# Two transformer blocks in float32 on one core: the RWKV stage in finer parts and another order

## The reference

```python
feat = feat + (prev - feat) * mu
r, k, v, wl, al, gl = jnp.split(feat, splits, axis=-1)
w = -jax.nn.softplus(-(w0 + jnp.tanh(wl) @ w2)) - 0.5
a = jax.nn.sigmoid(a0 + al @ a2)
g = jax.nn.sigmoid(gl) @ g2
kk = heads(k * k_k);  kk = kk * lax.rsqrt(jnp.sum(kk * kk, -1, keepdims=True) + 1e-12)
k = k * (1.0 + (a - 1.0) * k_a)
decay = jnp.exp(-jnp.exp(heads(w)))
def step(state, inp):
    sa = jnp.einsum('bhvk,bhk->bhv', state, -kk_t)
    state = state * d_t[:, :, None, :] + sa[..., None] * b_t[:, :, None, :] + v_t[..., None] * k_t[:, :, None, :]
    return state, jnp.einsum('bhvk,bhk->bhv', state, r_t)
# y: group norm, lnx_g, lnx_b, plus bonus = sum(r * k * r_k) * v, all times g
x = x + jnp.concatenate([mla_out, rw_out], axis=-1) @ w_o
```

## Time and profile before

| | |
|---|---|
| median of three runs | 2431.26 us |
| the profiled execution | 2428.68 us |
| its span, first to last instruction | 2426.8 us |
| mean granted clock of TensorE | 0.985 |
| busy: PE, DVE, ACT, POOL | 95%, 51%, 31%, 27% |
| chain that ended last: PE, DVE, DMA, issue, ACT | 82%, 8%, 4%, 3%, 2% |
| granted clock by fortieths of the span, in tenths | 9, but 8 in the sixth to eighth |

### The profile page before, as it was taken

How to read it: one execution, slowest core, us unless ns; L and a number is a source line. 1 busy time by engine, 2 the same in 40 slices (tenths; PEclk the granted TensorE clock), 3 DMA queues, 4 the chain that set the end, 5 groups by cost and what they waited for, 6 DMA issues and landing times.

```text
span 2426.8 us, 30979 instructions
## 1 busy us (share of the span) xinstructions
PE 2313.5 (95%) x12570; PEld 1658.2 (68%) x12570; DVE 1229.6 (51%) x2164; ACT 758.4 (31%) x1194; POOL 649.4 (27%) x288
## 2 busy tenths in 40 slices
PE   8989787798999999999999999999999999999999
PEld 3334555565444487678878888878767887888887
DVE  4454555535565623864466776111386346667610
ACT  3344222222111234442233333223444223333311
POOL 0000000011000033234444444444323444444443
PEclk9999988899999999999999999999999999999999
DMA  5431000028999832123333333223212333333322
GB/s 219 133 80 35 19 2 2 2 86 309 408 409 409 329 98 78 53 61 96 96 95 96 96 97 99 78 95 114 78 53 61 97 98 92 96 96 99 100 80 94
DMA packets 77789, 287.52 MB, mean 118 GB/s; under 512 B 6960, under 2 KB 7984, under 8 KB 77008
## 3 DMA queue, kind: packets, MB, share of 16 engines
q1 hardware_dynamic: 74512, 279.27, 33.9%
q0 software_dynamic: 1152, 4.19, 0.4%
q10 hardware_dynamic: 1984, 2.06, 0.3%
HBM read 277.83 MB, written 16.06 MB: 121 GB/s over the span
## 4 chain that ended last, share of the span: by engine, by line
PE 82%; DVE 8%; DMA 4%; issue 3%; ACT 2%; ACTq 0%; SPq 0%; POOL 0%; DVEq 0%; another core or an unknown queue 0%
PE bank L1974 12%; PE bank L1976 12%; PE bank L1975 12%; PE bank L551 5%; DMA arena<-in_stream 4%; PE bank L2123 3%; PE bank L2124 3%; PE bank L2122 3%; DVE arena L416 3%; PE bank L1583 2%; PE bank L1551 2%; PE bank L895 2%; PE bank L1959 2%; PE bank L1961 2%; PE bank L1960 2%
## 5 line engine op out<-in xcount | busy, mean ns | idle before, releaser
L1709 POOL TENSOR_TENSOR ring_low<-ring,W_high 128x1024 fp32r<-128x1024 f32 x252 | 606.2, 2406 | 1117.3 <-ACT W_high L426 1117.3
L1974 PE MATMUL bank<-H_high,W_high 128*128 128x512 f32 x1408 | 555.5, 394 | 7.9 <-ACT arena L426 5.9
L426 ACT ACTIVATE W_high<-ring 128x1024 fp32r<-128x1024 f32 x264 | 279.8, 1060 | 862.3 <-PE bank L1976 552.5
L1976 PE MATMUL bank<-H_high,ring_low 128*128 128x512 f32 x1408 | 548.5, 390 | 0.0
L1975 PE MATMUL bank<-H_low,W_high 128*128 128x512 f32 x1408 | 548.2, 389 | 0.0
L1974 PEld LDWEIGHTS bank<-H_high,W_high 128*128 128x128 f32 x1408 | 264.2, 188 | 77.9 <-issue 23.2
L1975 PEld LDWEIGHTS bank<-H_low,W_high 128*128 128x128 f32 x1408 | 264.4, 188 | 55.9 <-issue 1.9
L1976 PEld LDWEIGHTS bank<-H_high,ring_low 128*128 128x128 f32 x1408 | 264.3, 188 | 55.8
L416 DVE TENSOR_TENSOR arena<-bank,root 128x512 f32<-128x512 f32 x116 | 79.7, 688 | 295.9 <-PE bank L1976 295.7
L426 ACT ACTIVATE arena<-bank 128x512 f32<-128x512 f32 (+4 forms) x183 | 79.4, 445 | 315.3 <-PE bank L860 118.8
L422 DVE SCALAR_TENSOR_TENSOR arena<-arena 128x512 f32<-128x512 f32 (+3 forms) x64 | 118.0, 1844 | 99.1 <-ACT arena L430 98.4
(11 more groups left out here) (280 smaller groups left out, 3230.8 us busy)
## 6 DMA issues: line engine op xcount, KB each, us to landing
ring<-in_stream SPq DMA_DIRECT2D x288, 512.0 KB, 3.6
arena<-in_stream SPq DMA_DIRECT2D x31, 2048.0 KB, 12.8
arena<-in_stream SPq DMA_DIRECT2D x31, 1024.0 KB, 10.1
sorted_x<-in_zero_row SPq DMA_DIRECT2D x4, 2048.0 KB, 12.6
arena<-sorted_x SPq DMA_DIRECT2D x15, 512.0 KB, 16.3
X<-in_x SPq DMA_DIRECT2D x2, 1024.0 KB, 7.9
ring<-in_stream SPq DMA_DIRECT2D x1, 2048.0 KB, 19.4
out<-X SPq DMA_DIRECT2D x8, 256.0 KB, 6.9
```

The costliest lines, as they stand in the source:

```text
L426: return S.activation(o, i, f)
L1709: return G.tensor_tensor(ring_low[:, slot, :], ring[:, slot, :], W_high[:, s % 2, :].bitcast(F32), ALU.subtract)
L1974: mm(ps[:, :], wh[:, k, :], H_high[:, k, :], start=k == 0, stop=False)
L1976: i = mm(ps[:, :], wl[:, k, :], H_high[:, k, :], start=False, stop=k == KD - 1)
```

## The change

The parts are cut finer, and all engines follow a new order. "rows" keeps `ru`, `ra`, the square of KK and KK. New parts: "decay" (sum of KK's squares and the exponentials; LW, the running sum and its difference on DVE), "mix" (A, B, KP), "root" (two products), "factors" (AT, BT), "late" (YB, RT, KT), "first" (the blocks abT and ab), "second" (ak, br, kr), "masks" (MT, TI with its identity sum, then TT with its own), "hats" (BH, KH, DC), "others" (the six masks of ak, br, kr). "bonus", with the gate, and "turned", with the values, come behind "grow 2". YB moves to the buffer GS. The latent tiles are spread 4, 2, 1, 1 over the preparations, in pieces of two k-steps; tile 6 also takes k-step 4, tile 7 k-steps 4 and 5, so that six early pieces go. The scan's parts follow named parts of the preparation, and the output of pair c comes behind "read" of pair c + 1. ACT asks for its tanh tables at the end of "read".

```diff
+LATENT = {0: (0, 1, 2, 3), 1: (4, 5), 2: (6,), 3: (7,)}
+WITH_LATENT = {6: 5, 7: 6}
+def latent_pieces(c):
+    for m in LATENT[c]:
+        last = WITH_LATENT.get(m, 4)
+        yield "latent", m, (0, 1)
+        yield "latent", m, tuple(range(2, last))
 def rwkv_prepare(c):
-    for part in ("rows", "root", "bonus", "turned", "blocks", "keyed"):
-        yield part, c, 0
-    for lev in LEVELS:
-        yield "cross", c, lev
-        yield "grow", c, lev
-    yield "read", c, 0
+    piece, land = latent_pieces(c), iter(LATENT[c])
+    parts = ["rows", "latent", "decay", "latent", "mix", "root", "factors", "landed", "late", "first", "second", "masks",
+             ("cross", 2), "hats", "others", ("grow", 2), "bonus", "turned", "keyed"]
+    if c == 0:
+        parts = ["rows", "decay", "latent", "latent", "mix", "latent", "latent", "root", "landed", "latent", "latent", "factors", "landed",
+                 "late", "first", "second", "landed", "masks", ("cross", 2), "hats", "others", ("grow", 2), "bonus", "turned",
+                 "latent", "latent", "keyed"]
+    for lev in LEVELS[1:]:
+        parts += [("cross", lev), ("grow", lev)]
+        if lev == 4 and c == 0:
+            parts += ["landed"]
+        if lev == 4 and c == 1:
+            parts[-1:] = ["latent", ("grow", 4), "latent"]
+        if lev == 8 and c == 1:
+            parts[-1:] = ["landed", ("grow", 8)]
...
-BESIDE = "pss" * 4 + "ps" * 10 + "pspp"
+STEPS_BEHIND = ["rows", "decay", "mix", "root", "factors", "late", "others", ("grow", 2), "turned", "keyed", ("cross", 4), ("grow", 4),
+                ("cross", 8), ("grow", 8), ("cross", 16), ("grow", 16)]
+NORM_BEHIND = {("cross", 32): ("mean",), ("grow", 32): ("spread",), "read": ("output",)}
-EARLY_PIECES = [(m, k, x) for m in range(8) for k in (4, 5, 6) for x in range(2)]
-EARLY_AFTER = {("cross", 3, 32): 2, ("grow", 3, 32): 2, ("read", 3, 0): 2, ("state", 3, NCH - 1): 2, ("mean", 3, 0): 4}
+EARLY_PIECES = [(m, k, x) for m in range(8) for k in range(WITH_LATENT.get(m, 4), 7) for x in range(2)]
+EARLY_PIECES[4:8] = EARLY_PIECES[6:8] + EARLY_PIECES[4:6]
+EARLY_AFTER = {("grow", 3, 32): 2, ("spread", 2, 0): 2, ("read", 3, 0): 2, ("state", 3, NCH - 1): 2, ("mean", 3, 0): 4}
+EARLY_AFTER["step", 3, 0] = EARLY_AFTER["state", 3, 1] = 2
...
-        W.update(YB=W["LW"], MT=W["LW"], TT=W["A"], ...
+        W.update(YB=W["GS"], MT=W["LW"], TT=W["A"], ...
...
             elif part == "read":                       # rwkv_act
...
+                if c < 3:
+                    exp_tanh_tables()
...
+            elif part == "factors":                    # rwkv_dve
+                dv.e.wait_ge(dv.chain, dv.n)
+                dv.e.wait_ge(*dv.nth("explog", c + 1))
+                stt(w["AT"], w["KK"], -1.0, w["ELX"], ALU.mult, ALU.mult).then_inc(dv.chained(), 1)
+                tt(w["BT"], w["B"], w["ENL"], ALU.mult).then_inc(dv.tells("factors"), 1)
+            elif part == "late":
+                dv.e.wait_ge(*dv.nth("scan", 2 * c + 2))
+                stt(w["YB"], r_, one("r_k"), w["KP"], ALU.mult, ALU.mult).then_inc(dv.tells("rkr"), 1)
+                tt(w[f"RT{q}"], r_, w["EL"], ALU.mult).then_inc(dv.chained(), 1)
...
+                tt(w["KT"], w["KP"], w["ENL"], ALU.mult).then_inc(dv.tells("late_factors"), 1)
...
+                if part == "masks":
+                    for hh in range(2):
+                        dv.e.wait_ge(*dv.filled(f"mabT{c}_{hh}"))
+                        masked("abT", "MT", "lower", hh).then_inc(dv.chained(), 1)
+                    for hh in range(2):
+                        dv.e.wait_ge(*dv.filled(f"mab{c}_{hh}"))
+                        masked("ab", f"TI{q}", "lev1", hh).then_inc(dv.takes(f"mab{c}_{hh}"), 1)
...
+                    tt(c64(w[f"TI{q}"]), c64(w[f"TI{q}"]), over("eye", NCH), ALU.add).then_inc(dv.tells("tinv"), 1)
+                    for hh in range(2):
+                        masked("abT", "TT", "lev1T", hh).then_inc(dv.takes(f"mabT{c}_{hh}"), 1)
...
+                    tt(c64(w["TT"]), c64(w["TT"]), over("eye", NCH), ALU.add).then_inc(dv.chained(), 1)
```

More of the change, by code:

```diff
@@ L9 @@
+import itertools
 from contextlib import ExitStack
@@ L158, in rwkv_order @@
     for c in range(3):
[L159 to L163, removed]
+        scan = rwkv_scan(c)
+        for segment in rwkv_prepare(c + 1):
+            yield from early(segment)
+            part = (segment[0], segment[2]) if segment[0] in ("cross", "grow") else segment[0]
+            for _ in range(STEPS_BEHIND.count(part)):
+                yield from early(next(scan))
+            for _ in NORM_BEHIND.get(part, ()):
+                yield from early(next(scan))
     for segment in rwkv_scan(3):
@@ L173, in rwkv_jobs @@
     if part == "early":
-        return [f"wq{c}"] if n == (4, 0) else []
-    return {"rows": [f"ru{c}", f"ra{c}", f"rg{c}", f"wp{2 * c}", f"rt{c}_v"], "root": [f"rkk{c}"], "bonus": [f"rb{c}", f"wp{2 * c + 1}"],
-            "turned": [f"rt{c}_{x}" for x in "bka"], "blocks": [f"m{x}{c}_{hh}" for x in PRODUCTS for hh in range(2)],
+        return [f"wq{c}"] if n == (WITH_LATENT.get(c, 4), 0) else []
+    if part == "latent":
+        return [f"wp{c}"] if n[0] == 0 else []
+    blocks = [f"m{x}{c}_{hh}" for x in PRODUCTS for hh in range(2)]
+    return {"rows": [f"ru{c}", f"ra{c}"], "decay": [f"rkk{c}"], "bonus": [f"rb{c}", f"rg{c}"], "late": [],
+            "mix": [], "root": [], "factors": [], "hats": [], "masks": [], "others": [], "landed": [],
+            "turned": [f"rt{c}_{x}" for x in "vbka"], "first": blocks[0:4], "second": blocks[4:],
             "keyed": [f"rwk{c}"], "cross": [f"ix{c}_{n}"], "grow": [f"iy{c}_{n}"] + ([f"iz{c}_{n}"] if n != 32 else []),
@@ L769, in rwkv_pe @@
                     turn_feature(pe, c, x, src)
-            elif part == "blocks":
-                for x, (l_, r_) in PRODUCTS.items():
+            elif part in ("first", "second"):
+                pe.e.wait_ge(*pe.nth("factors" if part == "first" else "late_factors", c + 1))
+                for x, (l_, r_) in list(PRODUCTS.items())[0:2] if part == "first" else list(PRODUCTS.items())[2:]:
                     left, right = W[l_], W[f"RT{q}"] if r_ == "RT" else W[r_]
@@ L1255, in rwkv_dve @@
         def rwkv_dve(dv, part, c, n):
-            if part == "early":
+            if part in ("early", "latent"):
                 return
+            if part == "landed":
+                return add_latent_half(dv, c)
             q, w = c % 2, W
@@ L1271, in rwkv_dve @@
                 tt(w["ELX"], w["L"], w["LW"], ALU.subtract).then_inc(dv.tells("scan"), 1)
+            elif part == "mix":
                 dv.e.wait_ge(*dv.taken(f"ra{c}"))
@@ L1314, in rwkv_dve @@
+                for x, o, mask in (("ak", "MK", "upper"), ("br", f"MB{q}", "upper_eq"), ("kr", f"MR{q}", "upper_eq")) if part == "others" else ():
                     for hh in range(2):
```

107 lines of the change are left out of this document (56 added, 51 removed).

## The result

The kernel after takes a median of 2407.49 us (2407.18 to 2407.67 in four runs), the kernel before, run beside it, 2429.82 us (2427.98 to 2433.9): a ratio of 0.9905, interval 0.9889 to 0.9920. The profiled executions have spans of 2426.8 and 2405.3.

The account below looks back on a forecast made before the run. The bound was taken to be the order in which each engine does its part, not PE's or DVE's work alone. Terms +6.5 - 4.7 - 6.3 - 5.4 - 2.2 = -12.1 gave 2419.2 us, own range 2412 to 2426, widest 2403 to 2434.

Parts of the forecast that it names:

- Clock: Each period, 20 to 27 us behind "read": PE's pauses bring the lower clock onto the chain, 4.0 more (bounds 0 and 10).
- the sum: Whole stage: first preparation +6.5, periods -4.7, -6.3 and -5.4, end of the scan -2.2, together -12.1 us.
- The walk: New order of one period followed item by item with profiled durations: at the full clock 56.5 us for 65.2.
- in all +1.0: Second and third period: the output's DVE instructions, now behind "read" ahead of KK, delay the chain by 1.0 (bounds 0, 2.2).
- First preparation: Before the first "read": two more latent tiles make it 6.5 us longer (bounds 0 and +10); cross 4 starts at 292.1.
- for a longer low clock: Allowance of 0.8 us in the preparation before the first "read", part of its +6.5.
- End: Last scan: output placed before step 0 costs +1.3, eight fewer early pieces give -3.5; -2.2 us in all.
- the two waits of 3.4 and 5.5: Front of a period: PE's waits for DVE's step copy and for the X add were to go.
- rival 4: ACT loads its tables once more before the tanh: 1.28 in three periods, +3.8, so 2423 us; chance 0.06.
- Rival 1: The clock holds, no lower level in the new order: -24.9, so 2406 us; chance 0.20.
- Rival 2: Low clock spreads over the front, "read" to cross 4, at a mean of 0.64: +11.7, so 2443 us; chance 0.12.
- Rival 3: Gains cancel: first preparation +9, low clock about twice as long (7 us, not 4, each period): -0.6, 2431; chance 0.16.

Follow-up runs that it names:

- another order above: Kernel after with even latent tiles, scan steps in pairs, products uncut, and hats, bonus and turned ahead of the blocks: 2430.98 us, ratio to before 0.9992.
- with fillers: Kernel after plus matmuls on constants in PE's waits (3 products ahead of step 2, 4 behind br, 6 ahead of step 3): 2400.46 us, ratio to before 0.9878.
- undoing four edits together: Kernel after with even latent tiles, paired scan steps, uncut products, and hats, bonus, turned ahead of the blocks: 2430.98 us, periods 195.4.

## Why the prediction was wrong, point by point

**The step that failed is "Clock. ... So I expect the lower level around 20 to 27 ...: 4.0 more."** It put 12.0 on three periods. The lower level did come, in all three, and in the first for longer than the step said (13.8 us, then 6.5 and 6.7, for the 7 forecast). But its cost, taken by what its removal gains, is 2.8, 1.5 and 1.5, in all 5.8 (at least): 6.2 of the 12.1 by which the stage missed the sum. The step charged about 0.57 us for each us at the lower level; measured is 0.20 to 0.23 in this order (another order above comes to about 0.4). Much of the slow work lay beside DVE: the blocks took 3.93 for 128 matmuls, yet TI was ready within 0.1 of the time that it has at the full clock (17.7 with fillers). On the chain were cross 2, which ends 1.3 later than with fillers, and then step 3 and "grow 2", 1.5 more.

**The walk was too long behind "grow 2".** With the clock at 1.00 the first period is 54.9, where the walk had 56.5; the second 52.5 for 54.9, the third 54.6 for 55.8, in sum 5.2 (the 65.2 taken for all three periods of before was 0.4 too long in sum). Up to "grow 2" the walk was right: AT and BT 12.1 (11.6), TI 17.7 (17.4), the end of cross 2 20.2 (19.9), the adds 27.1 (27.1). From there to the end of "cross 4" it gave 7.3 and 6.7 was measured, and for the levels and "read" behind it 22.1, where 21.1 was measured: PE has hardly a pause there, and the walk sums single items, with their ends counted each time; that this is the reason was not tested. What the output's place in the second and third period cost ("in all +1.0") was not measured by itself.

**First preparation: +4.7 for +6.5.** Cross 4 started at 295.11 in the profile after; less the 4.0 of the MLA part that is 291.1, for 292.1 forecast. From there to "read" both kernels need the same 16.3 (286.33 to 302.61; 295.11 to 311.38). So 1.0 was the walk, and the 0.8 "for a longer low clock" was too much: behind an early mark, as in the profile before, the same code gives +4.3, and 0.4 is what the late mark adds.

```profile
295.11 1.10 PE L945 MATMUL bank<-arena 64*64 64x64 f32 x32
```

**End: -1.5 for -2.2.** The last spread begins 29.30 after "read" (27.72 before): +1.6 for +1.3 forecast. Behind it the projection starts 6.9 later (in which 0.21 is a wait for the last output) and no longer 10.0: -3.1 for -3.5. The last spread before, and after it the last spread and the projection after:

```profile
525.56 1.07 PE L880 MATMUL bank<-arena,cst 128*128 128x512 f32 x2
...
508.46 1.07 PE L930 MATMUL bank<-arena,cst 128*128 128x512 f32 x2
...
515.36 1.96 PE L718 MATMUL bank<-H,ring 128*128 128x512 f32 x4 [0.21 <-DVE H L457]
```

Right were the waits that go and the main ones that come: the two waits of 3.4 and 5.5 are gone, kr waits for the TT masks, the identity sum in front gains nothing, and ACT loads the tables that were asked for once (rival 4 did not happen):

```profile
312.80 1.28 ACT L477 ACT_TABLE_LOAD   x1
...
315.89 1.28 ACT L477 ACT_TABLE_LOAD   x1
```

**The rivals.** Rival 1 had the size nearly right (-24.9; the stage made -24.2), but not for its reason: the clock did not hold. Two errors in it cancel, so it came near by luck: 5.8 of clock that it left out and the 5.2 by which the walk was long. Rival 2 asked for a clock of 0.64 over the 34 us behind "read"; there it is 0.80, 0.90 and 0.90. Rival 3 asked for twice the stretch at the lower level: in the first period it came (13.8 us), but cost 2.8 and not 7.

The granted clock falls in every period of the kernel after, behind the pauses of PE for banks and copies, and comes back; it stays at 1.00 where the pauses are filled. The Trainium skill tells of a kernel in which short idle times of PE between groups of matmuls, cycling through the PSUM banks, make the clock go back and forth ("TensorE: Matmul & The Clock Gate", section "A second HAM failure mode: psum-queue depth-cycling"). The trace agrees that it happens here, between 1.00 and 0.50 in the windows above; what filling the pauses gains is 5.8 of 168, and the clock is not lost over the whole front, as the rival taken from that rule had it.

**What stays open.** Why undoing four edits together costs 27.6, when singly they cost 11.0, is shown for one wait and the start of the blocks in the first period, and in part by the clock of the third; the place of step 3 in that kernel was not tried by itself. The undone edits shift the low clock, so that what each is worth at an equal clock isn't known. Why the MLA part takes 249.4 or 253.5 was not tried.

## What to carry to other kernels

A stretch at the low clock costs what it adds to the chain, not what it adds to PE's busy time: walk the new order with the slow durations and let them wait beside the other engine, as with any other duration, before adding a lump. Edits of one order cover for each other, so test them undone together as well as singly; here cutting DVE's products was worth nothing alone, cost 4.7 in two periods beside another place for kr, and was one of the four edits whose undoing together lost 27.6. Matmuls on constants pay only where PE really waits; in an order whose waits lie elsewhere the same ones cost nearly twice what they had gained.

## What had not been expected of the hardware

The same MLA code, ahead of any change, came to its last sum at 249.3 to 249.6 or at 253.1 to 254.0, with a granted clock of 1.00 or 0.91 in 225 to 250: 4 us, more than most single edits here are worth. And 26 matmuls on constants in a period, at three places, held a granted clock of 1.00 over 162 us of an order that has a mean of 0.92 (0.88, 0.94, 0.94) without them.
